# An eight-core hybrid decoder layer on Trainium2: planning the order in eleven passes, gate rows by way of DRAM, and the last tiles by halves

## The reference

```
mod = silu(c) @ w_ada + b_ada                # sh1, sc1, g1, sh2, sc2, g2, 1024 each
h = rmsnorm(x, norm_mix_g) * (1 + sc1) + sh1
proj = h @ w_in                              # 1440 columns
y_mla = mla_group(...)    # 8 heads, dense causal, low-rank q and kv, rotary part
y_swa = swa_group(...)    # 8 heads, window 128, ALiBi, a sink per head
x = x + g1 * (concat([y_mla, y_swa]) @ w_o)
h = rmsnorm(x, norm_mlp_g) * (1 + sc2) + sh2
u = square(relu(h @ w_up))                   # 4096 wide
x = x + g2 * (u @ w_down)
return rmsnorm(x, final_g)
```

## Time and profile before

| | |
|---|---|
| time, median of 3 runs | 765.85 us (764.91 to 768.96) |
| the profiled execution | 765.9 us |
| its span, slowest core | 764.4 us (core 1; others 758.2 to 762.5) |
| TensorE busy | 713.9 us, 93% |
| VectorE, ScalarE, GpSimd busy | 555.5, 450.1, 232.9 us |
| mean granted clock of TensorE | 0.993 to 0.998 |

### The profile page before, as it was taken

One profiled execution on the slowest core, in us unless ns is written; L12 is line 12 of the kernel. 1 busy time (PEld: TensorE's weight loads), 2 busy tenths in 40 slices (PEclk: granted clock), 3 DMA queues, 4 the chain that ended last, 5 costly groups with the idle time before them and its releaser, 6 DMA issues.

```text
span 764.4 us, 17786 instructions; the slowest of 8 cores (758.2 to 764.4 us)
## 1 busy us (share of the span) xinstructions
PE 713.9 (93%) x5970; PEld 447.4 (59%) x5970; DVE 555.5 (73%) x982; ACT 450.1 (59%) x753; POOL 232.9 (30%) x210
## 2 busy tenths in 40 slices
PE   0679999999899999999999989999999999999996
PEld 0344556556556555554666647766667766676652
DVE  3587978744673556649999686777878678779987
ACT  2136826777679888884755604664446544565655
POOL 2020136766573443331233411233124343000000
PEclk9999999999999999999999999999999999999999
DMA  8999892699814957999975896525943886704115
GB/s 193 235 211 192 226 177 55 135 153 141 129 44 117 219 139 195 262 264 270 263 180 175 233 232 119 208 96 158 239 171 103 215 223 181 202 16 192 52 61 220
DMA packets 77801, 131.81 MB, mean 172 GB/s; under 512 B 40592, under 2 KB 48400, under 8 KB 75536
## 3 DMA queue, kind: packets, MB, share of 16 engines
q1 hardware_dynamic: 67776, 97.05, 43.0%
q0 software_dynamic: 9936, 33.62, 27.2%
HBM read 119.71 MB, written 29.10 MB: 195 GB/s over the span
## 4 chain that ended last, share of the span: by engine, by line
PE 87%; DMA 7%; issue 2%; DVE 2%; POOL 1%; ACT 1%; DVEq 0%; ACTq 0%; POOLq 0%
PE ps L998 27%; PE ps L1702 23%; PE ps L1927 22%; PE ps L1408 7%; PE ps L1432 4%; DMA arena<-wada 4%; DMA arena<-wup 4%; PE ps L1454 2%; PE ps L1478 1%; PE ps L1096 1%; PE ps L1293 1%; DVE arena L1084 0%; DVE arena L1136 0%; ACT arena L1458 0%; DVE arena L1161 0%
## 5 line engine op out<-in xcount | busy, mean ns | idle before, releaser
L998 PE MATMUL ps<-arena 128*128 128x512 bf16 (+2 forms) x1484 | 248.2, 300 | 20.8 <-DMA arena<-wada 16.4
L1702 PE MATMUL ps<-arena 128*128 128x256 bf16 x1680 | 199.6, 273 | 3.4 <-DMA arena<-wup 2.9
L1927 PE MATMUL ps<-arena 128*128 128x512 bf16 x840 | 197.1, 381 | 0.0
L1702 PEld LDWEIGHTS ps<-arena 128*128 128x128 bf16 x1680 | 163.4, 98 | 41.8 <-issue 9.7
L998 PEld LDWEIGHTS ps<-arena 128*128 128x128 bf16 x1484 | 105.5, 98 | 105.9 <-issue 29.5
L1416 ACT ACTIVATE arena<-ps 128x1024 bf16<-128x1024 f32 (+1 forms) x160 | 138.1, 896 | 47.2 <-PE ps L1408 21.4
L1890 DVE TENSOR_TENSOR arena<-ps,arena 128x512 f32<-128x512 f32 x194 | 128.1, 685 | 18.9 <-PE ps L1927 14.5
L1615 POOL TENSOR_TENSOR arena<-arena 128x512 bf16<-128x512 f32 x64 | 81.6, 1288 | 194.3 <-DVE arena L1827 75.1
L1927 PEld LDWEIGHTS ps<-arena 128*128 128x128 bf16 x840 | 82.6, 98 | 83.6 <-issue 2.9
L1688 DVE TENSOR_TENSOR arena<-ps,arena 128x512 f32<-128x512 f32 x90 | 61.7, 689 | 49.7 <-PE ps L1702 35.6
L1827 DVE TENSOR_TENSOR arena<-arena 128x1024 bf16<-128x1024 bf16 (+1 forms) x108 | 94.4, 887 | 4.2 <-DMA arena<-wup 2.9
(11 more groups left out here) (106 smaller groups left out, 601.9 us busy)
## 6 DMA issues: line engine op xcount, KB each, us to landing
arena<-hss SPq DMA_DIRECT2D x12, 1792.0 KB, 7.8
arena<-x SPq DMA_DIRECT2D x32, 512.0 KB, 8.7
arena<-wdn SPq DMA_DIRECT2D x64, 256.0 KB, 5.8
arena<-wada POOLq DMA_DIRECT2D x24, 512.0 KB, 11.2
arena<-wup POOLq DMA_DIRECT2D x16, 512.0 KB, 13.5
out<-arena SPq DMA_DIRECT2D x15, 512.0 KB, 2.7
hss<-arena SPq DMA_DIRECT2D x4, 1792.0 KB, 7.8
x1s<-arena SPq DMA_DIRECT2D x12, 512.0 KB, 6.5
```

The lines of the kernel that those rows point to most:

```text
L998: S.op("pe", lambda h, i=i: h.matmul(out, lhsT=lhs_list[i], rhs=rhs_list[i], start=(i == 0), stop=(i == n - 1)), r=rbufs[i], w=[bankb[bank]])
L1702: S.op("pe", lambda h, k=k, c0=c0, fc=fc, wv=wv, hv=hv, b=b, first=first: h.matmul(bk(b, None, (fc * 256, fc * 256 + 256)), lhsT=wv[:, k, ...
L1927: S.op("pe", lambda h, f=f, av=av, wv=wv, p=p, b=b, first=first, n=n, key=key: h.matmul(bk(b), lhsT=av[:, f, p * 128:(p + 1) * 128], rhs=w ...
```

## The change

1. `Sched.plan` runs the list scheduler eleven times. The first pass uses the priorities of before. After each pass `latest` goes back from the planned end and gives each instruction a latest start; `mixed` makes new priorities of a times the rank by that and 1 - a times the old value, with a from `MIX_`. The pass with the earliest planned end is repeated as the eleventh and is what runs.
2. REFILL_OFF goes from 400 to 200.
3. `load_gate` is now one fp32 matmul that turns eight columns of MODCOL into 8 rows of 128, a copy of 8x128, a write of it to DRAM and a read that spreads the row over all partitions.
4. The shift's first w_ada block waits for x tile 9 instead of 8.
5. `load_mix` waits for the fold of a slice of w_o: in group 0 the read of quarter n for the fold of slice n, in group 1 all four for slice 4.
6. Tiles 14 and 15 go by halves. The inverse root takes the first half's sum (with eps) as the bias of its Ln, so no addition stands behind the second half's square; the products with final_g go into buffers of their own, and tile 15's instructions get a lower priority value by LAST_OFF.

```diff
-REFILL_OFF = 400
+REFILL_OFF = 200
...
+LAST_OFF = 40
+HALVES = 14
+ROUNDS = 10
+MIX_ = (0.4, 0.45, 0.55, 0.6, 0.65, 0.8)
...
-    def schedule(self):
-        import heapq
+    def plan(self):
...
+        deps = [list(o.deps) for o in self.all]
+        pri = first = [o.pri for o in self.all]
+        best = None
+        for k in range(ROUNDS + 1):
+            if k == ROUNDS:
+                pri = best[1]
+            for o, d, p in zip(self.all, deps, pri):
+                o.deps, o.pri, o.taken = list(d), p, False
+                for t in o.tens:
+                    t.i, t.left = None, len(t.ops)
+            try:
+                self.schedule()
+            except RuntimeError:
+                self.makespan = None
+            if self.makespan is not None and (best is None or self.makespan < best[0]):
+                best = (self.makespan, pri)
+                late = self.latest()
+            pri = self.mixed(first, late, k)
+
+    def latest(self):
+        after = [[] for _ in self.all]
+        for o in self.all:
+            for (d, dv, kind) in o.deps:
+                after[d.idx].append(o)
+        nxt = {}
+        for e in self.ENGS:
+            for a, b in zip(self.ops[e], self.ops[e][1:]):
+                nxt[a.idx] = b
+        late = [0.0] * len(self.all)
+        for o in sorted(self.all, key=lambda o: -o.start):
+            t = self.makespan
+            for x in after[o.idx]:
+                t = min(t, late[x.idx] - (0.0 if x.eng == o.eng and not o.dma else self.LAT[x.eng] if not o.dma else 0.0))
+            t -= (o.npk * o.pk + 2100.0) if o.dma else o.dur + (165.0 if o.eng == "pe" else 0.0)
+            if o.idx in nxt:
+                t = min(t, late[nxt[o.idx].idx] - o.dur)
+            late[o.idx] = t
+        return late
+
+    def mixed(self, first, late, k):
+        n = sorted(range(len(late)), key=lambda i: late[i])
+        rank = [0] * len(late)
+        for r, i in enumerate(n):
+            rank[i] = r
+        a = MIX_[k % len(MIX_)]
+        return [a * r + (1 - a) * p for r, p in zip(rank, first)]
+
+    def schedule(self):
...
-            wada_load(c, [bXT[0]] if c == 0 else [])
+            wada_load(c, [bXT[1]] if c == 0 else [])
...
         def load_gate(i):
             dst, bdst = ((G1B, bG1), (G2B, bG2))[i]
             c0 = (16, 40)[i]
-            for half in range(2):
-                b = take_bank(RB)
-                for c in range(4):
-                    j = c0 + half * 4 + c
-                    S.op("pe", lambda h, j=j, c=c, b=b: h.matmul(
-                        bk(b, None, (c * 128, c * 128 + 128)), lhsT=MODCOL[:, j:j + 1].to_broadcast([128, 128]), rhs=IDENTF,
-                        start=(c == 0), stop=(c == 3)), r=[bMOD[j // 2], bIDFB], w=[bankb[b]])
-                S.op("act", lambda h, half=half, b=b: h.activation(out=dst[:, half * 512:(half + 1) * 512], in_=bk(b), func=AF.Copy),
-                     r=[bankb[b]], w=[bdst])
+            b = take_bank(RB)
+            S.op("pe", lambda h: h.matmul(bk(b, (0, 8), (0, 128)), lhsT=MODCOL[:, c0:c0 + 8], rhs=IDENTF, start=True, stop=True),
+                 r=bMOD[c0 // 2:c0 // 2 + 4] + [bIDFB], w=[bankb[b]])
+            S.op("act", lambda h: h.activation(out=GROW, in_=bk(b, (0, 8), (0, 128)), func=AF.Copy), r=[bankb[b]], w=[bGROW])
+            S.dma("sp", lambda h: h.dma_start(out=gate_d[i].rearrange("(a b) -> a b", a=8, b=128), in_=GROW), bGD[i], r=[bGROW], w=[bGD[i]])
+            S.dma("sp", lambda h: h.dma_start(out=dst, in_=bcast_row(gate_d[i:i + 1, :], D)), bdst, r=[bGD[i]], w=[bdst])
...
             S.dma("sp", lambda h: h.dma_start_transpose(out=MIXT[mt], in_=mx_d[G, quad]), bMIXT[mt],
-                  r=[bMXD[G][quad]], w=[bMIXT[mt]])
+                  r=[bMXD[G][quad]] + ([bWO[quad]] if G == 0 else [bWO[4]] if G == 1 else []), w=[bMIXT[mt]])
...
-                        if t == 15:
+                        if t >= HALVES:
                             final_half(t, half)
-                    if t < 15:
+                    if t < HALVES:
                         final_tile(t)
...
+        def final_parts(t):
+            st = ctr["fst", t] = nxt_of("sta", 4)
+            gained = {}
+
+            def mean_sq(half):
+                hs = slice(half * 512, (half + 1) * 512)
+                S.op("act", lambda h: h.activation(out=JUNK[:, hs], in_=X1[t][:, hs], func=AF.Square, scale=float(D) ** -0.5,
+                                                   accum_out=STA[st][:, half:half + 1]), r=[bX1[t][half]], w=[bSTA[st][half], bJUNK])
+
+            def gain(half):
+                hs = slice(half * 512, (half + 1) * 512)
+                v, bv = gained[half] = (WST[half], bWST[half]) if t == 15 else (RT[half], bRT[half])
+                S.op("dve", lambda h: h.tensor_tensor(out=v, in0=X1[t][:, hs], in1=FGB[:, hs], op=ALU.mult),
+                     r=[bX1[t][half], bFG], w=[bv])
+
+            def root():
+                S.op("act", lambda h: h.activation(out=STA[st][:, 3:4], in_=STA[st][:, 1:2], func=AF.Ln, bias=STA[st][:, 2:3]),
+                     r=[bSTA[st][1], bSTA[st][2]], w=[bSTA[st][3]])
+                S.op("act", lambda h: h.activation(out=STA[st][:, 4:5], in_=STA[st][:, 3:4], func=AF.Exp, scale=-0.5),
+                     r=[bSTA[st][3]], w=[bSTA[st][3]])
+
+            def eps_up():
+                S.op("act", lambda h: h.activation(out=STA[st][:, 2:3], in_=STA[st][:, 0:1], func=AF.Identity, bias=EPSC),
+                     r=[bSTA[st][0], bEPS], w=[bSTA[st][2]])
+
+            def scale_out(i, half, c0, c1, engs):
+                g, bg = gained[half]
+                v = g[:, c0:c1]
+                bo = Buf(f"o{t}_{i}")
+                fd = lambda h: h.tensor_scalar(out=v, in0=v, scalar1=STA[st][:, 4:5], scalar2=None, op0=ALU.mult)
+                fa = lambda h: h.activation(out=v, in_=v, func=AF.Copy, scale=STA[st][:, 4:5])
+                fs = {"dve": fd, "act": fa}
+                S.flex({e: fs[e] for e in engs}, r=[bg, bSTA[st][3]], w=[bo])
+                return bo
+
+            def store(half, bs):
+                g, bg = gained[half]
+                od = S.dma("sp", lambda h: h.dma_start(out=out_d[t * 128:(t + 1) * 128, 512 * half:512 * half + 512], in_=g),
+                           bFIN[(2 * t + half) % 4], r=bs + [bg])
+                S.final.append(od)
+
+            return mean_sq, gain, root, eps_up, scale_out, store
+
         def final_half(t, half):
...
             if half == 0:
...
+                ctr["fp", t] = final_parts(t)
+            mean_sq, gain, root, eps_up, scale_out, store = ctr["fp", t]
+            if t == 15:
+                S.prio(-LAST_OFF)
+            mean_sq(half)
             if half == 0:
...
+                eps_up()
+            gain(half)
+            if half == 1:
+                root()
+                if t == 15:
+                    store(0, [scale_out(0, 0, 0, 512, ("dve",))])
+                    store(1, [scale_out(1, 1, 128, 512, ("act",)), scale_out(2, 1, 0, 128, ("dve",))])
+                else:
+                    for i in range(2):
+                        store(i, [scale_out(i, i, 0, 512, ("act", "dve"))])
+            S.prio(0)
...
-        S.schedule()
+        S.plan()
```

More of the change, by code:

```diff
@@ L289, in schedule @@
                 o.dur = self.estimate(o)
+        deps = [list(o.deps) for o in self.all]
[43 more added lines that the diff above has]
+    def schedule(self):
+        import heapq
         tenants = {id(t): t for o in self.all for t in o.tens}
@@ L977, in build_program @@
         JUNK, bJUNK = put("junk", WDN[0][1, 0][1][0].alloc.lo, [128, D], BF16, "E")
+        a = AR.put("GROW", E7 + 16384, 512, "ADB")
+        GROW, bGROW = AR.ap(a, [8, 128], F32), Buf("GROW", a)
+        bGD = [Buf(f"gd{i}") for i in range(2)]
         V_E0 = a_V[0].lo // 2
@@ L1947, in final_half @@
         def final_half(t, half):
-            hs = slice(half * 512, (half + 1) * 512)
             if half == 0:
-                ctr["fst"] = nxt_of("sta", 4)
-            st = ctr["fst"]
-            S.op("act", lambda h: h.activation(out=JUNK[:, 0:512], in_=X1[t][:, hs], func=AF.Square,
-                                               accum_out=STA[st][:, half:half + 1]), r=[bX1[t][half]], w=[bSTA[st][half], bJUNK])
-            S.op("dve", lambda h: h.tensor_tensor(out=X1[t][:, hs], in0=X1[t][:, hs], in1=FGB[:, hs], op=ALU.mult),
-                 r=[bX1[t][half], bFG], w=[bX1[t][half]])
@@ L1956, in final_half @@
-            if half == 0:
-                return
-            S.op("dve", lambda h: h.tensor_tensor(out=STA[st][:, 2:3], in0=STA[st][:, 0:1], in1=STA[st][:, 1:2], op=ALU.add),
-                 r=[bSTA[st][0], bSTA[st][1]], w=[bSTA[st][2]])
-            rstd4(st, 2, 1, D)
-            bo = [Buf(f"o{t}_{i}", bX1[t][0].alloc) for i in range(2)]
-            S.op("dve", lambda h: h.tensor_scalar(out=X1[t][:, 0:512], in0=X1[t][:, 0:512], scalar1=STA[st][:, 10:11],
```

(9 more changed lines are left out.)

## The result

The changed kernel took 756.29 us (median of four runs) against 765.55 for the kernel before: a ratio of 0.9863, 95% interval 0.9823 to 0.9903, about 10.5 us. Three of its runs took 754.64 to 756.73; the fourth, 772.5, is of a kind that both kernels have, in which cores of one die show a lower granted clock than the others, and such runs are left out of every comparison here. A later repeat gave 0.9837 (0.9799 to 0.9875). Forecast were 755.4 us, 747 to 763, faster.

A forecast was written before the change was run, and what follows sets the result against it. TensorE (PE), busy nearly everywhere, was taken as the bound. Core 5, then slowest: 761.2 - 3.9 - 0.8 - 1.0 - 1.6 = 753.9, plus 1.5 from span to execution time gives 755.4 us; range 747.0 to 763.0.

The forecast's parts named there:

- Gate rows: Gate matmuls on PE: 32 trace rows become 4, saving 3.9 us on every core.
- rival 3: First fold of w_o: the gate row comes late and POOL stands up to 7 us; 764.1 or 770.5 us, chance 0.12.
- Transposes behind the folds: PE's "issue" stand at 191.5 on core 1: reads waiting for folds let PE's instructions through, saving 4.5 us there.
- rival 1: Stand in 190 to 200: not the transposes' making, or they repeat it later; 4.5 us back, at worst 759.9, chance 0.15.
- Order of the up weights: PE's wait for up weights near 457: needed blocks load first, saving 4.6 us on core 1, 0.8 core 5, 2.9 core 7.
- rival 2: Up weights: VectorE stands for them instead of PE; price 4.7 us, giving 760.1, at worst 763, chance 0.11.
- Start: PE's wait for a scaled x tile at 56.37: two squares move to ScalarE, saving 1.0 us; later shift weights cost 0.
- End: Behind the last half's square: Ln starts without waiting for VectorE's addition of the two sums, saving 1.6 us.
- Eleven passes: Whole order: another pick with the same work, costed at 0; opening one wait would cost 3 + 1.7 us.
- The slowest core: Core 5, keeping waits of its own, becomes slowest at 753.9 us; core 1 falls to 748.8.
- rival 4: All cores: other chance waits vanish too and every core nears core 1's sum, about 749 to 750 us, chance 0.05.

The follow-up runs named there:

- e11: Changed kernel, order kept, each gate's matmul issued eight times in a row instead of once; ratio 0.9889 to the kernel before.
- e10: Changed kernel run again unaltered, as control for e9, e11 and e12 on the same chip; ratio 0.9837 to the kernel before.
- e2: Kernel before with only REFILL_OFF changed from 400 to 200; ratio 0.9954 to the kernel before.
- e3: Kernel before with only the new end, tiles 14 and 15 by halves and the first sum as Ln's bias; ratio 0.9982.
- e8: Kernel before with only the eleven scheduler passes; ratio 0.996 to the kernel before.
- e9: Kernel before with each transposing read of group 0 issued twice into the same buffer, otherwise in its order; ratio 0.9997.
- e1: Kernel before with only the transposing reads of attention output made to wait for folds of w_o slices; ratio 0.9987.
- e6: Changed kernel, order kept, but the transposing reads no longer wait for folds; ratio 0.9867 to the kernel before.
- e12: Changed kernel with slices 4 to 7 of w_o loaded behind the first gate's copy, planned again; ratio 0.9957 to the kernel before.
- e4: Changed kernel with one scheduler pass instead of ten and a pick; ratio 0.9963 to the kernel before.
- e5: Changed kernel, order kept, with the shift's first weight load waiting for x tile 8 again; ratio 0.987 to the kernel before.
- e7: Changed kernel with the old gate (16 fp32 matmuls and four copies for each gate), planned again; ratio 0.9859 to the kernel before.

## Why the prediction was right, step by step

Three small slips in the rows, which change nothing: the last square's accumulator was read at 758.46, not 758.55; the fold in the earlier trace rows took 2.15 us, not 2.13; and 249.1 is 49 us behind 200.44, not 47.

- **Gate rows, -3.9:** right; 3.9 by e11 against e10 in the mean span (3.1 to 4.7), 4.0 by the time. The row landed 5.5 to 9.3 us behind its matmul, under most of the estimate of 9 to 16, and POOL never waited for it, so rival 3 had nothing to work with.
- **Transposes behind the folds, -4.5 on core 1:** the stand went, and the reading of it is supported but not proven; its place in the change was wrong.
  For it: in the fourteen traces PE stands 23 times by "issue" for 1 us or more behind 60 us, and each time the DMA share of the ten microseconds ahead was 0.95 or more (up to 1.32). With a share of 0.99 to 1.22 in 180 to 200 (before, e2, e3, e8, e9), 12 of 40 cores stood there; in the nine other traces, with 1.00 or less, none of 72. e1, where only SP's queue differs from before, has q8's packets earlier, no stand, and a mean span shorter by the expected amount.
  Against it: full engines do not suffice, as 28 of those 40 cores, e1 and e6 behind 195, and e9 show; and behind 270 us there is no such stand at all, though 1180 of 5264 ten-microsecond windows there have a share of 1.0 or more. What decides which core stands is open. The rule of the Trainium skill ("Runtime: NRT & Kernel Launch", "Instruction fetch mechanics") that the fetch is mostly hidden fits these traces as "mostly": where a stand came, the engines were full.
  What failed is the sentence that the wait for folds does it: e6 has no such wait and no stand, so SP's new order does. The reads also began 19 us later on core 1, not some 15. And rival 1 came half true: a stand of the same kind turned up at 171 on cores 0 and 6, where the share is 1.06 too. (e12 has none there, but the changed order as it stood in five traces has 6 in 40 cores, so that is too few to tell.)
- **Order of the up weights, -0.8 to -4.6:** right, the wait is gone on every core; 3.5 us of time in e2, 2.8 of mean span. VectorE asked earlier and waited 0.3 us on one core at most: rival 2 fell, as the blocks went out 24 us earlier and not 5.
- **Start, -1.0:** the wait of PE's transposes for scaled tiles went from 12.3 to 11.4 us on core 1. No run took this part alone. The shift weights cost 0 on most cores, 0.4 on core 4, and 1.4 to 1.5 us before 60 on cores 0 and 6, inside the bounds of 0 to 2.3.
- **End, -1.6:** right in its mechanism and a little too large. From the end of VectorE's last sum to the end of the span it took 6.8 us before and 5.6 with the change, on average over the cores: 1.3 less. Ln comes 1.6 us earlier behind the square, but the square itself starts 0.3 instead of 0.15 us behind that sum, since ScalarE adds eps to the first half's sum in between.
- **Eleven passes, 0:** this step failed. I priced every edit against the order of before, as if none made a new wait. In one pass they do (e4), and the edits then bring 2.8 us instead of 10.5. The passes bring 3.1 us alone (2.1 of mean span) and about 8 on top of the edits; they repair what the others broke. The sum came out right because the pick that was made has hardly a wait of that kind; e12 shows that the same ten passes can also end with one. Measured one at a time, the parts e1, e2, e3 and e8 and the gate of e11 add up to 11.0 us of mean span, about what the whole has (9.9 and 11.4); e4 shows that they do not simply add.
- **The slowest core:** 753.9 was forecast for core 5 with its own stand at 380. That stand is gone, core 5 has 748.8, and core 6 has 753.1 for its stand at 171. Cores 1, 2, 5 and 7 all came near core 1's forecast sum of 748.8 (748.4 to 749.5), which is the level of rival 4, at a chance of 0.05. That 755.4 still fits is in part luck: a stand that was not foreseen took the place of one that went. In e10 two of three runs, 752.4 and 752.7, lie between the forecast and rival 4's 749 to 750.

## What to carry to other kernels

Where a scheduler sets the order, an edit's price is that of the edit plus that of the new plan: to measure a part, keep the order and change a wait or the work in place (e5, e6, e11), or the plan's luck (e7, e12) is what is measured. With eight cores the time is the slowest one's, so sum the cores separately, look for waits that all share, and do not count on stands that one or two have by chance, neither as a gain to be had nor as a loss that stays. The average span over all cores and runs told a 3.9 us part apart (e11) where the intervals of the time overlapped. A stand by "issue" is worth reading against the DMA share and the instruction queue of the microseconds ahead of it.

## What the runs showed of the hardware

The granted clock differs between cores that run the same program with the same waits. In the changed kernel's start every core stands 2.52 or 2.53 us for the same scaled tile and goes on at 42 to 45; in 40 to 60 us core 3 then has 0.83, cores 1, 4 and 7 have 0.91, and the rest 1.00. Between 0.83 and 1.00 lie up to 3.4 us of work in 20, as an estimate, and that is larger than most terms of the sum; the spans of cores 3 and 5 are 2.7 us apart (first core 3, then core 5):

```profile
40.00:60.00 20.00, 17.32 (x137) 10.06 (x135) 14.99 (x32) 8.39 (x26) 5.07 (x9) 0.83 0.92 182
```

```profile
40.00:60.00 20.00, 16.82 (x165) 9.63 (x163) 17.10 (x39) 7.64 (x23) 5.00 (x9) 1.00 1.00 192
```

I had counted a clock loss only behind stands of core 1 and not that the other cores may lose more in the start. In the kernel before it is so too behind the wait for up weights: core 1 stood 2.94 us and has 0.83 in 455 to 465, core 7 stood 2.93 and has 1.00. So a stand of some 3 us costs 4.5 on one core and 3 on another. The cause of the difference stays open.
